# Block inverses of the delta rule: level 1 on all four TensorE quadrants, half-width products, one corner tile; another VectorE order in the first mixer

## The reference

```python
lower = jnp.where(strict, jnp.einsum('nhcid,nhcjd->nhcij', kb, k) * decay, 0.0)
rhs = jnp.concatenate([v * beta[..., None], kb * jnp.exp(gc)[..., None]], axis=-1)
uw = lax.linalg.triangular_solve(lower, rhs, left_side=True, lower=True, unit_diagonal=True)
...
def step(state, inp):
    u_c, w_c, qk_c, qg_c, kd_c, a_c = inp
    v_new = u_c - jnp.einsum('nhik,nhkv->nhiv', w_c, state)
    o = jnp.einsum('nhik,nhkv->nhiv', qg_c, state) + jnp.einsum('nhij,nhjv->nhiv', qk_c, v_new)
    state = state * a_c[..., None, None] + jnp.einsum('nhjk,nhjv->nhkv', kd_c, v_new)
    return state, o
```

## Time and profile before

| | us |
|---|---|
| median of three runs | 3120.95 |
| the profiled execution | 3121.05 |
| its span in the trace | 3118.9 |
| PE (TensorE matmul) busy | 3070.9 (98%) |
| PEld (weight load) busy | 2620.3 (84%) |
| DVE (VectorE) busy | 1886.4 (60%) |
| ACT (ScalarE) busy | 1308.3 (42%) |
| share of PE in the chain that ended last | 91% |

### The profile page before, as it was taken

How to read it: one execution, slowest core, us unless ns; L and a number is a source line. 1 busy time by engine, 2 the same in 40 slices (tenths; PEclk the granted TensorE clock), 3 DMA queues, 4 the chain that set the end, 5 groups by cost and what they waited for, 6 DMA issues and landing times.

```text
span 3118.9 us, 52126 instructions
## 1 busy us (share of the span) xinstructions
PE 3070.9 (98%) x20820; PEld 2620.3 (84%) x20820; DVE 1886.4 (60%) x2769; ACT 1308.3 (42%) x2221; POOL 97.3 (3%) x106
## 2 busy tenths in 40 slices
PE   9999999999999999999999999999999999999999
PEld 8897889889878988888788888788887888876899
DVE  6745674674458656766776566467734776346444
ACT  5443454554345452222465566432224222244433
POOL 0000000000000020000000000100000000000000
PEclk9999999999999999999999999999999999999999
DMA  7543554554435544454322000235522444220453
GB/s 268 183 159 125 189 188 162 185 183 159 176 136 188 175 149 160 179 201 163 134 82 81 2 3 3 95 148 189 202 95 90 181 188 175 94 81 28 149 182 128
DMA packets 62484, 441.19 MB, mean 141 GB/s; under 512 B 6768, under 2 KB 8944, under 8 KB 9328
## 3 DMA queue, kind: packets, MB, share of 16 engines
q1 hardware_dynamic: 60992, 437.39, 38.2%
q10 hardware_dynamic: 1328, 1.46, 0.1%
HBM read 437.77 MB, written 1.05 MB: 141 GB/s over the span
## 4 chain that ended last, share of the span: by engine, by line
PE 91%; DVE 4%; ACT 3%; issue 1%; DMA 0%; POOL 0%; DVEq 0%; ACTq 0%; SPq 0%; POOLq 0%
PE ps_high L544 46%; PE ps_low L544 43%; PE ps_low L553 1%; PE ps_high L553 1%; ACT sb_w_split L797 1%; DVE sb_w_split L834 0%; DVE sb_arena L2177 0%; DVE sb_x_split L2940 0%; ACT sb_arena L2848 0%; DVE sb_silu L2958 0%; ACT sb_xn L2839 0%; DMA sb_ring<-weights 0%; DVE sb_rinv L4703 0%; ACT sb_xn L4076 0%; ACT sb_sq L4070 0%
## 5 line engine op out<-in xcount | busy, mean ns | idle before, releaser
L797 ACT ACTIVATE sb_w_split<-sb_ring 128x2048 fp32r<-128x2048 f32 x260 | 498.5, 1917 | 890.5 <-PE ps_low L544 697.5
L834 DVE TENSOR_TENSOR sb_w_split<-sb_ring,sb_w_split 128x2048 fp32r<-128x2048 f32 x260 | 597.6, 2298 | 257.0 <-ACT sb_w_split L797 257.0
L544 PE MATMUL ps_low<-sb_x_split,sb_w_split 128*128 128x512 f32 (+1 forms) x3520 | 691.3, 354 | 7.9 <-DVE sb_w_split L834 4.0
L544 PE MATMUL ps_high<-sb_x_split,sb_w_split 128*128 128x512 f32 (+1 forms) x3520 | 686.9, 353 | 0.3 <-DVE sb_w_split L834 0.3
L544 PEld LDWEIGHTS ps_low<-sb_x_split,sb_w_split 128*128 128x128 f32 x3520 | 578.9, 189 | 107.9 <-DVE sb_x_split L2940 6.3
L544 PEld LDWEIGHTS ps_high<-sb_x_split,sb_w_split 128*128 128x128 f32 x3520 | 580.4, 189 | 94.6 <-DVE sb_w_split L834 0.6
L544 PE MATMUL ps_low<-sb_a_split,sb_w_split 128*128 128x256 f32 (+1 forms) x2112 | 370.2, 325 | 0.0
L544 PE MATMUL ps_high<-sb_a_split,sb_w_split 128*128 128x256 f32 (+1 forms) x2112 | 365.8, 323 | 0.0
L544 PEld LDWEIGHTS ps_low<-sb_a_split,sb_w_split 128*128 128x128 f32 x2112 | 314.3, 190 | 37.6 <-DVE sb_w_split L834 2.5
L544 PEld LDWEIGHTS ps_high<-sb_a_split,sb_w_split 128*128 128x128 f32 x2112 | 314.9, 190 | 30.9
L1047 DVE SCALAR_TENSOR_TENSOR sb_rest<-sb_ring,sb_consts 128x1024 f32<-128x1024 f32 x256 | 313.3, 1224 | 27.1 <-DVE sb_rest L1047 7.7
(11 more groups left out here) (411 smaller groups left out, 3057.1 us busy)
## 6 DMA issues: line engine op xcount, KB each, us to landing
sb_ring<-weights SPq DMA_DIRECT2D x412, 1024.0 KB, 4.8
sb_consts<-consts SPq DMA_DIRECT2D x1, 2148.0 KB, 18.6
sb_sq<-xT SPq DMA_DIRECT2D x1, 1024.0 KB, 5.8
sb_ring<-weights SPq DMA_DIRECT2D x2, 512.0 KB, 7.8
sb_h<-ctxT ACTq DMA_DIRECT2D x1, 1024.0 KB, 17.4
out<-sb_h SPq DMA_DIRECT2D x1, 512.0 KB, 3.0
sb_vectors<-vectors ACTq DMA_DIRECT2D x1, 269.0 KB, 5.9
out<-sb_h SPq DMA_DIRECT2D x1, 256.0 KB, 2.7
```

What stands on the lines that cost most here:

```text
L544: ins = self.g.nc.tensor.matmul(out, lhsT, rhs, start=start, stop=stop)
L797: g.nc.scalar.activation(g.w_split[:, 0, s % 2, :], g.ring[:, n % SLOTS, :], ACT.Copy).then_inc(g.sem["w_high"], 1)
L834: g.nc.vector.tensor_tensor(g.w_split[:, 1, s % 2, :], g.ring[:, n % SLOTS, :], g.w_split[:, 0, s % 2, :].bitcast(F32), ALU.subtract).then ...
```

## The change

In the delta steps:

- Level 1 uses the interleaved groups too. `first_level` writes into a tile `start` that holds the identity from the beginning: three predicated copies (128x256 for direction 0, two of 64x256 for direction 1, whose halves change places) instead of two multiplications and two additions. The tile is filled with the identity once before the first step, and the clearing of `inv_t` goes.
- `both_products` multiplies the blocks only with the half of the columns that `both_changed` reads: 64x32 instead of 64x64, and `to_product` copies 128 columns instead of 256.
- The corner products of both directions land in one low tile, copied by one ScalarE copy. The transposes are copied in four copies over all 128 partitions, each scaled by a column of ones and zeros, which writes zeros where `inv_t` must be zero. TensorE's final corner products wait only for the corner copy and the first two of these, and go into one joint tile, which VectorE frees after its second copy. `new_values` of both directions wait for that.
- `key_values` of direction 1 moves from before level 4's changed products to behind them.

In the first block's mixer the keys' rotated rows are kept twice over 128 partitions with zeros in the other half, so that all score products run over 128 rows; VectorE clears the zero halves once per layer and adds the rotation in two half-partition instructions. VectorE takes all four maxima and scales heads 0 and 1 before `head_out(0)`, and the Fourier bias comes after it.

```diff
@@ mix1_tensor, mla_scores
-        base = 64 * (h % 2)
...
-            pe.mm(out, b["q_rot"][base:base + 64, h // 2, q * P:(q + 1) * P], b["k_rot"][base:base + 64, :],
-                  False, True, full="low" if q == 1 else None)
+            pe.mm(out, b["q_rot"][:, h // 2, q * P:(q + 1) * P], b["k_rot"][:, h % 2, :], False, True, full="low" if q == 1 else None)
@@ mix1_vector
     dve.skip("low", 2)
-    head_out(0)
+    dve.tiles["high"] += 1
+    dve.wait_ge(g.sem["high_free"], dve.freed["high"])
+    dve.foreign["high"] = False
     read += [peak(2), peak(3)]
     scale(0, read[0])
+    scale(1, read[1])
+    dve.wait_ge(g.sem["root"], dve.due("root"))
+    dve.engine.sem_inc(g.sem["high_free"], dve.frees("high"))
+    head_out(0, freed=True)
     for p in range(2):
...
-    scale(1, read[1])
     transposed_probs(0)
@@ delta_step_tensor
     def both_products(level, tiles):
...
-                    pe.mm(tiles[d][landing(rows, d), block(h)], of_step(b, "blocks", s)[rows, d, block(h)], b["inv"][rows, d, block(h)],
+                    pe.mm(tiles[d][landing(rows, d), quarter(h)], of_step(b, "blocks", s)[rows, d, block(h)],
+                          changed_half(b["inv"][rows, d, block(h)], level, d),
                           full="low" if h == GH - 1 and rows == HIGH_HALF else None)
...
-    for d in range(2):
-        pe.wait_ge(g.sem["inv_start"], pe.due("inv_start"))
-        start_transposes(d)
+    pe.wait_ge(g.sem["inv_start"], pe.due("inv_start", 2))
+    both_transposes("start", open_two("low"))
...
-    for d in range(2):
-        pe.wait_ge(g.sem["low_free"], started - 1 + d)
-        first_products(d)
-        product_in[d] = pe.tiles["low"]
+    pe.wait_ge(g.sem["low_free"], started)
+    both_products(1, open_two("low"))
+    products_in = pe.tiles["low"]
     if s:
         new_values(pe, b, p, 1)
-    for d in range(2):
-        pe.wait_ge(g.sem["low_free"], product_in[d])
-        first_changed(d)
+    tiles = open_two("joint")
+    pe.wait_ge(g.sem["low_free"], products_in)
+    both_changed("start", tiles)
...
-        if level == 4 and values:
-            key_values(pe, b, p, 1)
         if level in (4, 5):
...
+        if level == 4 and values:
+            key_values(pe, b, p, 1)
         if level == 5 and not first:
             state_products(0)
...
-    tiles = open_two("joint")
-    pe.wait_ge(g.sem["low_free"], inverse_in)
+    pe.room("joint")
+    tile = pe.open("joint")
+    pe.wait_ge(g.sem["low_free"], corners_in)
+    pe.wait_ge(g.sem["far_in"], pe.due("far_in", 2))
@@ new_values
-    pe.wait_ge(g.sem["joint_free"], JOINTS * p + JOINTS - 1 + d)
+    pe.wait_ge(g.sem["joint_free"], JOINTS * (p + 1))
@@ delta_step_scalar
-    for d in range(2):
-        far = corner(d)[1]
-        act.wait_ge(g.sem["low_full"], act.tiles["low"] + 1)
-        A(b["product"][far, d, 0:GH * HALF], act.tile("low")[far, 0:GH * HALF], ACT.Copy).then_inc(g.sem["low_free"], act.frees("low"))
+    act.wait_ge(g.sem["low_full"], act.tiles["low"] + 1)
+    A(b["product"][:, 0, 0:GH * HALF], act.tile("low")[:, 0:GH * HALF], ACT.Copy).then_inc(g.sem["low_free"], act.frees("low"))
+    turned = []
     for d in range(2):
...
+        turned.append(heads_view(act.tile("low")[:, 0:GH * HALF]))
+        far = corner(d)[1]
+        A(corner_heads(b["inv_t"], slice(0, P), d, far), turned[d], ACT.Copy, scale=rows_of(g, far)).then_inc(g.sem["far_in"], act.adds("far_in"))
+    for d in range(2):
+        near = corner(d)[0]
+        A(corner_heads(b["inv_t"], slice(0, P), d, near), turned[d], ACT.Copy, scale=rows_of(g, near)).then_inc(g.sem["low_free"], act.frees("low"))
@@ first_level
+    v.copy_predicated(heads_view(b["start"][:, 0, :]), pairs.to_broadcast([P, GH, HALF]),
+                      heads_view(of_step(b, "blocks", s)[:, 0, :])).then_inc(g.sem["inv_start"], dve.adds("inv_start"))
+    for rows in (LOW_HALF, HIGH_HALF):
+        to = landing(rows, 1)
+        ins = v.copy_predicated(heads_view(b["start"][to, 1, :]), pairs[rows, :, :].to_broadcast([HALF, GH, HALF]),
+                                heads_view(of_step(b, "blocks", s)[rows, 1, :]))
```

More of the change, by code:

```diff
@@ L2223, in mix1_vector @@
     step(v.memset(b["m_x"][:, :, TOK + 2:TOK + 4], 0.0))
+    for i, rows in enumerate((HIGH_HALF, LOW_HALF)):
+        step(v.memset(b["k_rot"][rows, i, :], 0.0))
     plain_rinv_vector(dve)
@@ L3476, in closing, with changed_half, quarter, rows_of @@
     return s > 0 and s % 2 == 0
-def changed_half(ap, level, d, name):
-    later = (name == "inv_t") != (d == 1)
-    return ap.rearrange("p (b two s) -> p b two s", two=2, s=1 << level)[:, :, int(later), :]
+def changed_half(ap, level, d):
+    return ap.rearrange("p (b two s) -> p b two s", two=2, s=1 << level)[:, :, d, :]
+def quarter(h):
+    return slice(h * HALF // 2, (h + 1) * HALF // 2)
 def corner(d):
     return (LOW_HALF, HIGH_HALF) if d == 0 else (HIGH_HALF, LOW_HALF)
+def rows_of(g, half):
+    return g.const("head_ones")[:, half.start:half.start + 1]
 def corner_heads(buffer, rows, d, cols):
@@ L3632, in open_two, with both_transposes @@
         return [pe.open(side), pe.open(side)]
[L3634 to L3645, removed]
-        tile = pe.open("low")
-        for h in range(GH):
-            for rows in (LOW_HALF, HIGH_HALF):
-                pe.mm(tile[rows, block(h)], of_step(b, "blocks", s)[rows, d, block(h)], b["inv"][rows, d, block(h)],
-                      full="low" if h == GH - 1 and rows == HIGH_HALF else None)
-    def first_changed(d):
-        pe.room("joint")
-        tile = pe.open("joint")
-        for h in range(GH):
-            for rows in (LOW_HALF, HIGH_HALF):
-                changed = changed_half(b["product"][rows, d, block(h)], 1, d, "inv")
-                pe.mm(tile[rows, h * HALF // 2:(h + 1) * HALF // 2], b["turned"][rows, d, block(h)], changed,
-                      full="joint" if h == GH - 1 and rows == HIGH_HALF else None)
-    def both_transposes(tiles):
+    def both_transposes(source, tiles):
         for h in range(GH):
@@ L3682, in both_changed @@
                 for rows in (LOW_HALF, HIGH_HALF):
[L3683 to L3684 removed]
+                    pe.mm(tiles[d][landing(rows, d), quarter(h)], b[turned][rows, d, block(h)], b["product"][rows, d, quarter(h)],
                           full="joint" if h == GH - 1 and rows == HIGH_HALF else None)
@@ L3789, in delta_step_tensor @@
             near, far = corner(d)
-            pe.mm(tiles[d][near, block(h)], b["product"][far, d, block(h)],
-                  corner_heads(b["inv_t"], far, d, far)[:, h, :], full="joint" if h == GH - 1 else None)
+            pe.mm(tile[near, block(h)], b["product"][far, 0, block(h)],
+                  corner_heads(b["inv_t"], far, d, far)[:, h, :], full="joint" if (h, d) == (GH - 1, 1) else None)
     if next_pair(s):
@@ L4198, in delta_vector @@
             blocks_part(dve, b, 0, KEYS0_AT.index(n))
+    for d in range(2):
+        v.tensor_copy(heads_view(b["start"][:, d, :]), all_heads(g.const("block_identity"))).then_inc(g.sem["vec_step"], dve.adds("vec_step"))
     first_level(dve, b, 0)
-    v.memset(b["inv_t"], 0.0).then_inc(g.sem["vec_step"], dve.adds("vec_step"))
     dve.begin_steps()
```

72 lines of the change are left out of this document (35 added, 37 removed).

## The result

The changed kernel takes 3103.96 us (median of five runs, 3099.89 to 3104.24) against 3120.70 before: a ratio of 0.9945, 95% interval 0.9931 to 0.996, or 16.7 us less. Five more runs of it gave 3101.48 against 3120.22, 0.994 (0.9927 to 0.9954), 18.7 us less. The forecast was 3101.5, 19.6 less. The spans of the two profiled executions lie 21.1 us apart; the experiment "again" says why that is too much.

What follows compares the result with a forecast made beforehand. The prediction took TensorE's queue and its idle waits to bound the kernel, with memory and clock out of it in the delta steps. Terms 6.9 + 7.3 + 0.5 + 2.9 + 2.0 = 19.6 us from 3121.05 gave 3101.5, range 3095 to 3110.

Steps and rivals of the forecast that it cites:

- End of a step: Eight delta steps: TensorE's wait for the last ScalarE copy before final corner products goes, 0.86 each, 6.9 us (5.3 to 6.9).
- Level 1: Delta steps' level 1: three TensorE groups shorten from about 1.09 to 0.55-0.60, less new waits; 7.3 us (5.4 to 7.5).
- new_values behind VectorE's corner copies: Steps 2, 4, 6 and tail: new_values waits for VectorE's second corner copy, starting 1.72 after the final products.
- Shorter copies: ScalarE's 128-column product copies save about 0.24 where waited for, in step 4 and step 7's level 5: 0.5 us.
- Half width on TensorE: Level products of 64x32 instead of 64x64 gain nothing on TensorE: 0, bounds 0 and 2 us.
- key_values: Moved behind level 4's changed products, it covers the 0.67 idle before level 5: 2.9 us (2.6 to 2.9).
- Mixer: Both mixer layers: 128-row scores shorten but VectorE's run sets the end; 1.0 per layer, 2.0 us (-1 to 5.6).
- one sign of the forecast: Mixer: the output projection was to come 1 us nearer to the Fourier products.
- Copies bind: Rival: level 1 copies stay 0.67 a pair, masked copies 0.6 apart, mixer gives nothing: 3107.6 us, chance 0.18.
- Scores in full: Rival: the mixer's shorter score products count fully, 5.6 instead of 2.0 us: 3097.9, chance 0.14.
- Slower through predicated copies: Rival: first_level's predicated copies exceed their room of 0.52 each; at 1.6 each, 3127.5 us, chance 0.03.
- One bank serialises: Rival: final and corner products of both directions, writing one tile, run one after the other; 8 us back, 3109.5, chance 0.04.

Runs made afterwards that it cites:

- again: The changed kernel run once more with no edit: 3101.48 us, ratio 0.994.
- two_tiles: Changed kernel, but final corner products of the two directions go to two joint tiles and new_values waits only for its own direction's corner copy: 3099.44 us.
- values_back: Changed kernel with key_values of direction 1 ahead of level 4's changed products again: 3104.14 us, ratio 0.9947.
- scores_only: Changed kernel with 128-row rotary score products kept but VectorE's old order in the mixer: 3106.96 us, ratio 0.9958.
- six_copies: Changed kernel with ScalarE's six copies of 64 partitions again at each step's end, no masks, corner products into two low tiles: 3108.42 us.
- twice_predicated: Changed kernel with each of first_level's three predicated copies done twice, same data: 3107.40 us, ratio 0.9962.

## Why the prediction held, point by point

- **End of a step, 6.9 forecast, 7.3 measured** and 7.4 on taking it back. The last masked copy was to end 3.57 after the changed products; it ended 3.53 after them. The mean of a masked copy is 473 ns, as the exponentials of the earlier trace rows. The size was low because TensorE's own work was put at 3.94 with gaps and is 3.87, so that 0.93 came free in a step and not 0.86.
- **Level 1, 7.3 forecast, 6.5 measured** (6.98 and 0.04, less 0.51). After an odd step 0.65, 0.59 and 0.65 against 0.64: right, and by the forecast's path, since the changed products start 1789.42 - 1784.93 = 4.49 after the final products, 4.50 forecast. A pair of product copies took 0.46, 0.43 forecast. After an even step 1.34 against 1.46, and 1.08 in step 1. The term that was mis-sized is the path: I had ScalarE's product copies bind at 3.33 after the transposes. They don't: TensorE's own groups come to 0.63 + 1.09 + 0.60 + 1.13 = 3.45, since a group costs 0.04 to 0.08 more where the next has another form than my 0.55 and 1.09 have it. ScalarE is next to them: with copies 0.11 longer, level 2 came 0.21 later. The 0.12 between 3.45 and 3.33 is what steps 3, 5 and 7 fell short by. In step 1 a wait that I did not name appeared, 0.26 for the join, since the outputs of a first chunk have four instructions (0.71) and not eight as cover:
```profile
1765.71 0.71 PE L544 MATMUL ps_high<-sb_arena,sb_ring 128*128 128x128 f32 x4
1766.69 0.69 PE L544 MATMUL ps_low<-sb_consts,sb_xn 64*64 64x64 f32 x32 [0.26 <-DVE sb_xn L4319]
```
- **new_values behind VectorE's corner copies, 1.72 forecast:** 1.70, in steps 2, 4, 6 and the tail (1.71) only. That the changed kernel left this wait open is what "two_tiles" won.
- **Shorter copies:** 1.9 in level 1 and 0.5 elsewhere forecast; 1.5 and 0.8 measured, 2.34 for all. **Half width on TensorE:** 0 forecast, means of 217 against 220 ns measured.
- **key_values, 2.9 forecast, 2.12 measured** on taking it back, 2.30 in place. The 0.67 wait went, but I moved a group as if it cost the same anywhere. Between products and transposed keys it cost 1810.78 - 1809.78 = 1.00, and the products 0.57 before it:
```profile
1810.78 0.60 PE L553 MATMUL ps_low<-sb_consts,sb_arena 128*128 128x128 f32 x4
```
  Behind the changed products it costs 1803.86 - 1802.77 = 1.09, and the products 1801.47 - 1800.82 = 0.65 before another neighbour:
```profile
1800.82 0.62 PE L544 MATMUL ps_low<-sb_xn,sb_sq 64*64 64x32 f32 x32
1801.47 0.66 PE L553 MATMUL ps_low<-sb_consts,sb_arena 128*128 128x128 f32 x4
1802.18 0.67 PE L544 MATMUL ps_high<-sb_sq,sb_xn 64*64 64x32 f32 x32
1802.77 1.16 PE L544 MATMUL ps_high<-sb_ring,sb_arena 128*128 128x128 f32 x8
1803.86 0.69 PE L544 MATMUL ps_low<-sb_consts,sb_xn 64*64 64x64 f32 x32
```
  That takes 0.17 from each 0.67: 0.50, as "values_back" has it in steps 1 and 5.
- **Mixer, 2.0 forecast, 1.98 measured,** in kind by the reason given: the score products fell from 4.99 to 3.72, and VectorE's order decides what arrives. The fit of the size is partly luck. VectorE's run up to its last scaling was to end 0.5 earlier, and ends 0.32 earlier (20.51 after the first score products, 20.83 before); the copies behind it were to give about 0.5 and gave 0.67. And one sign of the forecast failed: the output projection is not 1 us nearer to the Fourier products but 0.47 farther (321.05 - 299.44 = 21.61, before 322.29 - 301.15 = 21.14). The 1.46 that the first pair of score products saves lies ahead of the Fourier products, and 0.47 of it is given back behind them. TensorE waited 0.81 for the exponentials, which the forecast had as the bound on the third score tile, then for the bias, as foretold, and for two copies of the turned probabilities (0.27 and 0.35), which were not:
```profile
316.34 0.62 DVE L2214 TENSOR_SCALAR sb_arena<-sb_arena 128x256 f32<-128x256 f32 x2
```
  (VectorE's last scaling before the change), and in the changed kernel:
```profile
299.44 3.62 PE L544 MATMUL ps_low<-sb_ring,sb_arena 128*128 128x256 f32 x16
...
304.30 3.72 PE L544 MATMUL ps_low<-sb_arena 128*128 128x256 f32 x16 [0.81 <-ACT sb_arena L1996]
...
314.10 0.63 PE L553 MATMUL ps_high<-sb_consts,sb_arena 128*128 128x128 f32 x4 [1.17 <-DVE sb_sq L2332]
...
315.77 0.62 DVE L2212 TENSOR_SCALAR sb_arena<-sb_arena 128x256 f32<-128x256 f32 x2
```
- **The rivals.** Copies bind, 3107.6: no, the masked copies were in time, a pair in 0.83 as forecast (0.37 + 0.47), and a pair of product copies takes 0.46 and not 0.67. The argument for it was half right: with half the columns a product copy's mean fell from 399 to 291 ns, not to half. Scores in full: no, 1.98 came and not 5.6, and "scores_only" got none of it. Slower through predicated copies: a copy is 0.45 and the room was nearly used up, since VectorE reaches to_rest 0.06 before the final products start (1784.87 and 1784.93). The breakpoint of 0.52 was about right, its price too high, because key products and length sums cover most or all of it ahead of steps 1, 3 and 5. One bank serialises: no, 0.62 against 0.61 for the final group ("two_tiles") and 1.09 against 1.09 for the corner group ("six_copies"). The Trainium skill, TensorEngine Tiling (Array Packing), Restrictions and Gotchas, has different row tiles unable to access one PSUM bank simultaneously; the measured groups decide against a cost of it here.
- **The sum.** 19.6 forecast, 18.3 by stages, 16.7 and 18.7 by medians. Level 1 and key_values were 1.4 too high and the end of a step 0.4 too low, so the errors partly cancel; the pause in step 2 took 0.5. That the profiled execution was "the median within 0.1" hid that it had one of the clock's drops, so a forecast against it was one against a typical execution, while the one profiled after was among the fastest.

## What to carry to other kernels

When a wait is taken out, add up TensorE's own groups with the durations that they have beside their new neighbours, not beside the old ones; two queues that end within about 0.1 us of each other leave no cover for either. A shorter product brings nothing if the engine that reads it runs without a gap: change that engine's order with it, and measure each half alone. Where totals of a kernel spread by 6 us and terms are 2, read the terms from windows of the changed stages.

## What the runs showed of the hardware

- In these executions the granted clock goes from 1.00 (2.4 GHz) to 0.50 (1.2 GHz) behind idle time of TensorE. Behind 2.21 to 2.23 us at 1518 to 1526 it fell in all 13 traces. Elsewhere it did not fall each time: after 3.04 us in layer 1 of "scores_only" and not after 3.04 in layer 0 of the same execution, after 2.50 ahead of step 0 in "twice_predicated", after 1.18 at 1151 in some executions and not in others. The drops that differ between executions cost 1.5 to 2.5 us each. So idle time that "costs only itself" may cost as much again or more.
- With moving data of 64x64 and of 64x32 a matmul instruction on a 64x64 tile takes 220 and 217 ns (mean).
- Sixteen such instructions from two array row halves into one PSUM bank, to partitions that don't overlap, take 0.62 us up to the next group, into two banks 0.61.
- A predicated copy of 128x256 takes 0.45 us, one of 64x256 0.444, and a ScalarE copy of 128x256 with a column as scale 0.473 against 0.38 without.
